# An expert's down weights read as one run per partition, with gate and up columns taken every fourth

## The reference, cut to what matters

```python
D_MODEL = 1024
D_EXPERT = D_MODEL // 2
...
    def expert_block(args):
        xblk, e = args
        hid = jax.nn.silu(xblk @ w_gate[e]) * (xblk @ w_up[e])
        return hid @ w_down[e]
```

## Time and profile before

| | before |
|---|---|
| median of 3 runs | 2670.03 us (2668.91 to 2671.3) |
| the profiled execution's own time | 2669.63 us |
| its span, first to last instruction | 2667.7 us |
| mean granted TensorE clock | 0.939 |
| busy PE / PEld | 2358.7 us (88%) / 1651.4 us (62%) |
| busy DVE / ACT / POOL | 838.9 (31%) / 435.9 (16%) / 481.8 us (18%) |
| DMA | 608.74 MB, 130511 packets, mean 228 GB/s |
| HBM read, written | 599.41 MB, 42.04 MB |

### The profile page before, as it was taken

How to read it: one execution, slowest core, us unless ns; L and a number is a source line. 1 busy time by engine, 2 the same in 40 slices (tenths; PEclk the granted TensorE clock), 3 DMA queues, 4 the chain that set the end, 5 groups by cost and what they waited for, 6 DMA issues and landing times. The chain is left out here.

```text
span 2667.7 us, 39347 instructions
## 1 busy us (share of the span) xinstructions
PE 2358.7 (88%) x15384; PEld 1651.4 (62%) x15384; DVE 838.9 (31%) x2103; ACT 435.9 (16%) x1079; POOL 481.8 (18%) x608
## 2 busy tenths in 40 slices
PE   4999879999299999999959997999489999999975
PEld 3999745565166666666638984555266666666642
DVE  1323345655601111011115665465611111011107
ACT  0010132321011111111101112222001111111111
POOL 0000003444111111111111111344111111111114
PEclk8999989999599999999979998899689999999997
DMA  9454420001397999999932103100189999999945
GB/s 357 148 177 145 181 94 26 24 17 48 131 369 296 391 399 392 389 391 395 369 114 100 48 33 117 59 17 24 57 356 384 384 381 393 386 389 381 372 191 202
DMA packets 130511, 608.74 MB, mean 228 GB/s; under 512 B 20608, under 2 KB 23680, under 8 KB 111984
## 3 DMA queue, kind: packets, MB, share of 16 engines
q1 hardware_dynamic: 112400, 569.61, 54.8%
q0 software_dynamic: 16864, 37.78, 3.8%
q10 hardware_dynamic: 1152, 0.03, 0.0%
HBM read 599.41 MB, written 42.04 MB: 240 GB/s over the span
## 5 line engine op out<-in xcount | busy, mean ns | idle before, releaser
L1888 PEld LDWEIGHTS gate_up<-room,w_gate_up 128*128 128x128 f32 x4608 | 522.6, 194 | 31.5 <-issue 31.5
L1888 PE MATMUL gate_up<-room,w_gate_up 128*128 128x128 f32 x4608 | 529.4, 277 | 3.1 <-DVE room L1795 3.1
L1897 PE MATMUL down<-w_down,room 128*128 128x512 f32 x576 | 256.8, 599 | 0.0
L1905 PE MATMUL gate_up_short<-w_gate_up,room 128*64 128x512 f32 x1152 | 255.1, 595 | 0.0
L1804 DVE TENSOR_TENSOR room<-room,gate_up 128x128 f32<-128x128 f32 x144 | 41.4, 287 | 599.3 <-ACT room L1823 599.3
L1905 PEld LDWEIGHTS gate_up_short<-w_gate_up,room 128*64 128x64 f32 x1152 | 79.5, 137 | 171.2 <-issue 171.2
L1897 PEld LDWEIGHTS down<-w_down,room 128*128 128x128 f32 x576 | 106.5, 190 | 123.0 <-issue 120.5
L1807 DVE TENSOR_TENSOR room<-room,gate_up_short 128x256 f32<-128x256 f32 x36 | 15.2, 421 | 495.1 <-ACT room L1829 495.1
L1515 POOL COPY rows_idx<-slot_token 128x1 int32 (+1 forms) x78 | 14.3, 183 | 792.6 <-PE rows_turned L1875 712.0
L1918 PE MATMUL down<-w_down,room 128*64 128x512 f32 x576 | 131.5, 598 | 11.9 <-ACT room L1831 11.9
L1337 PE MATMUL proj<-w_out,mixT 128*128 128x512 f32 x288 | 129.5, 592 | 0.0
(11 more groups left out here) (354 smaller groups left out, 3213.3 us busy)
## 6 DMA issues: line engine op xcount, KB each, us to landing
w_gate_up<-in_w_exp_gate SPq DMA_DIRECT2D x72, 2048.0 KB, 8.6
w_gate_up<-in_w_exp_up SPq DMA_DIRECT2D x72, 2048.0 KB, 13.3
w_down<-in_w_exp_down SPq DMA_DIRECT2D x72, 2048.0 KB
ada_w<-in_w_ada SPq DMA_DIRECT2D x48, 1024.0 KB, 7.1
h_rows<-h SPq DMA_DIRECT2D x18, 512.0 KB, 2.6
w_out<-in_w_out SPq DMA_DIRECT2D x2, 4096.0 KB, 14.1
w_in<-in_w_in SPq DMA_DIRECT2D x2, 3072.0 KB, 17.5
xn<-expert_rows SPq DMA_DIRECT2D x10, 512.0 KB, 4.0
```

The costliest lines, as they stand in the source:

```text
L1888: mm = nc.tensor.matmul(H[j % 2][:, o, :], wgu[0][:, o, k, j * P:(j + 1) * P], xT[0][:, k, :], start=k == 0, stop=k == KT - 1)
L1897: mm = nc.tensor.matmul(Y[:, h, :], hid[:, j, :], wd[0][:, j, h * 512:(h + 1) * 512], start=j == 0, stop=j == JT - 1)
L1905: mm = nc.tensor.matmul(Hs[c * HP:(c + 1) * HP, :, :], xT[1][:, k, :], wgu[1][:, :, k, c * 2 * P:(c + 1) * 2 * P], start=k == 0, stop=k == ...
```

## The change

```diff
@@ def weights(i), SyncE
-                        src = a["w_exp_down"][l][bass.ds(e, 1)].rearrange("a (j p) n -> p (a j) n", p=P)
+                        src = a["w_exp_down"][l][bass.ds(e, 1)].rearrange("a (p j) n -> p (a j) n", j=JT)
@@ TensorE, ahead of experts(i)
+                by_digit = lambda w: w.rearrange("p o (n j) -> p o j n", j=JT)
@@ experts(i), long part
-                                mm = nc.tensor.matmul(H[j % 2][:, o, :], wgu[0][:, o, k, j * P:(j + 1) * P], xT[0][:, k, :], start=k == 0, stop=k == KT - 1)
+                                mm = nc.tensor.matmul(H[j % 2][:, o, :], wgu[0][:, o, k, j::JT], xT[0][:, k, :], start=k == 0, stop=k == KT - 1)
@@ experts(i), short part
-                            mm = nc.tensor.matmul(Hs[c * HP:(c + 1) * HP, :, :], xT[1][:, k, :], wgu[1][:, :, k, c * 2 * P:(c + 1) * 2 * P], start=k == 0, stop=k == KT - 1)
+                            mm = nc.tensor.matmul(Hs[c * HP:(c + 1) * HP, :, :].rearrange("p o (j n) -> p o j n", j=2), xT[1][:, k, :], by_digit(wgu[1][:, :, k, :])[:, :, c * 2:(c + 1) * 2, :], start=k == 0, stop=k == KT - 1)
```

## The result

The changed kernel takes 3494.31 us (median of 4 runs, 3493.78 to 3497.61) against 2669.47 us before (4 runs on the same chip, 2667.54 to 2671.3): 1.310 times as long, 95% interval 1.308 to 1.312. I had forecast no change, with a range up to 2722 us. The loss is 825 us.

What follows compares the result with a forecast made beforehand. TensorE was taken to bound the experts' loop, with the DMA engines nearly full but in time. All terms were taken as 0 on 2669.6 us, giving a forecast of 2669.5 us, range 2660 to 2722 us.

Steps and rivals of the forecast that it cites:

- What bounds the kernel: Experts' loop: TensorE fills each 35.18 us turn, 36 turns in all; DMA engines nearly full but in time.
- The DMA term: Down-weight transfers without 4 KB cuts: between nothing and 21 us of transfer time saved, taken as nothing, since TensorE waits for none.
- the rival of a faster kernel: DMA engines did set the pace somewhere: up to 21 us gained, 2649 us; chance 7%.
- the rival's smaller version: Only a part of the possible gain from DMA transfers counts: 2660 us; within the 7% for a faster kernel.
- Weight loads of the long part: L1888, 4608 loads of every fourth float32: same pace as L1875's stepped loads, about 0.11 us each, so 0 added.
- The 1%: Chance that a tenth to a fifth of L1888's accesses collide with another stream or the DMA's writes.
- The upper end: L1888's loads at VectorE's 1.72 times: 10.4 us a turn, 376 us in all; 0 was taken instead.
- the ratio 1.72: VectorE reductions: 1.80 ns an element with 32-byte steps against 1.05 ns over neighbours.
- VectorE's price per element: 1.80 ns with 32-byte steps; at L1905 a pair would take 0.92 us, + 277 us in all.
- Moving operand of the short part: L1905, 1152 MATMUL with a stepped operand: 0 taken, after L1875's loads; upper end + 182 to + 277 us.
- The first rival: Moving port pays for each new line, at L1905 only: + 182 to + 277 us, say 2920 us; chance 16%.
- L1905 alone: Place given for a loss from paying per new line: only the short part's gate and up, 7.02 us a turn.

## Why the prediction was wrong

*What bounds the kernel.* Right, and it is why the loss is so plain: TensorE sets the turn, and each us that a turn grew was paid 36 times. The DMA term was right too: the DMA alone changed nothing (0.9994), 26,880 packets fewer where I had reckoned 27,600, and PE waited for no DMA between 750 and 1300 us. That also settles the rival of a faster kernel: the interval's lower end, 0.9983, is a gain of 4.5 us, where the rival's smaller version (2660) had 9.5.

*Weight loads of the long part.* This is the step that failed, and it is two thirds of the loss: + 561 us where I took 0. The 1% that I gave it was for accesses that collide; a price per line at this place had no chance at all in my list. I had set L1875 against VectorE and chosen it as "nearer by engine, kind and size". It is nearer by engine and size, but not by kind: a transpose is not a plain float32 product, and the counts that I had (16 L1875 instructions a turn for 16 transposes in the code, 128 of L1888 for 64 products) showed that TensorE does different things in the two. As a plain product the same operand costs 333 ns a load. Why a transpose is spared stays open; no run looked into it further than that its kind decides.

*The upper end.* I had put the loads' upper end at 376 us by the ratio 1.72. VectorE's price per element, which I used for L1905 only, would have given 128 x 1.80 = 0.230 us a load, + 0.117 x 128 x 36 = + 540 us. The price per line carries over between readers, the ratio doesn't, since it depends on what a neighbour costs there.

*Moving operand of the short part.* The first rival had place, mechanism and price: + 182 to + 277 us, measured + 271, within 6 us of what VectorE's 1.80 ns gave. I gave it 16%, because I let L1875 speak for this port as well. "L1905 alone" was wrong.

*The rule weighed there.* The Trainium skill, "Advanced Engine Details and Errata", section "SBUF Cachelines", was right: lines of 16 bytes, and slower with a single hit. These runs agree for both of TensorE's ports in plain float32 products, as VectorE's rows did, and "at least two hits" is where the table turns: with two hits a load costs 6% more, with one it doubles. The transposes at L1875 don't follow it: with one hit to a line they lost nothing at 32 bytes and 8% a load at 16 (209 ns for 194). Taken at both lines with VectorE's price the sum would have been 540 + 277 = + 817 us, against 825 measured.

*The range.* 2660 to 2722 let one row, L1875, carry both terms. If that row was wrong, both fell together, and I had given a loss beyond the range a chance of 16%, for one of the two alone. The upper ends of the bounds stood in my text, and the range didn't reach them. Even those two together, 376 + 277 = + 653 us, fall short of the 825, because the first went by the ratio.

## What to carry to other kernels

Before a step of more than 8 bytes goes into a TensorE operand of a plain float32 product, count its lines of 16 bytes: about 1.8 ns each (1.78 to 1.87 in these runs), against 0.88 ns for a neighbouring column, and check whether TensorE is the engine that waits for nobody. In this kernel steps belonged into transposes, where they cost nothing at 32 bytes and under a tenth at 16, or into the DMA, whose runs of 4 KB and of 16 KB took the same time here. And an instruction of the trace vouches for another only if it is of the same kind: its count per operation in the code tells.

## What the runs showed of the hardware that I had not expected

A transpose reads a stationary operand with 32-byte steps at the pace of neighbours (194 ns a load), a plain float32 product with the same operand at 333 ns. TensorE, with either operand of a plain product, and VectorE pay nearly the same for a new line, 1.78 to 1.87 and 1.80 ns. And slow loads can cost the clock as well: after 4 us of L1875 with matmuls of 64 columns behind loads of 331 ns, without an idle moment of PE, the mean granted clock over L1897 was 0.70, and that piece took 10.02 us for 7.13. Over the 30 us of slow loads at L1890 in the changed kernel it stayed at 1.00:

```profile
1021.00:1051.00 30.00, 30.00 (x129) 29.68 (x128) 0.87 (x3) 2.71 (x5) 1.03 (x1) 1.00 0.43 183
```

Why the clock fell in the one and not in the other, no run here shows.
